# Output projection with tokens on partitions and 512 moving columns, row-sum norm, and the gate's products on DVE instead of PE

## The reference, cut to what matters

```
shift, scale, gate = split(c @ w_ada + b_ada, 3)          # c is one row of 1024; gate is one row of 1024
h = rmsnorm(x, g_pre) * (1 + scale) + shift
z_ssm, xbc, dt_raw, q, kv, nsa_gate, z_att, merge_gate = split(h @ w_in)
y_ssm = mamba2_branch(z_ssm, xbc, dt_raw, ...) @ w_ssm_out
y_nsa = nsa_branch(q, kv, nsa_gate, z_att, ...) @ w_nsa_out
mg = sigmoid(merge_gate)
merged = mg[0] * y_ssm + mg[1] * y_nsa
out = merged @ w_out                                      # 256 x 1024 times 1024 x 1024
return x + gate * rmsnorm(out, g_post)
```

## Time and profile before

| | |
|---|---|
| time of the timed runs | 501.9 us median of 3 (501.90, 499.15, 501.99) |
| profiled execution, first to last instruction | 498.6 us |
| PE busy | 456.4 us (92%), 3742 instructions |
| PE weight load busy | 417.5 us (84%) |
| DVE busy | 338.7 us (68%) |
| ACT busy | 272.5 us (55%) |
| POOL busy | 241.5 us (48%) |
| DMA | 83.0 MB, mean 166 GB/s |
| w_raw fetches | 133 of 512 KB, median 3.5 us from issue to landing |

### The profile page before, as it was taken

How to read it: one execution, slowest core, us unless ns; L and a number is a source line. 1 busy time by engine, 2 the same in 40 slices (tenths; PEclk the granted TensorE clock), 3 DMA queues, 4 the chain that set the end, 5 groups by cost and what they waited for, 6 DMA issues and landing times.

```text
span 498.6 us, 10047 instructions
## 1 busy us (share of the span) xinstructions
PE 456.4 (92%) x3742; PEld 417.5 (84%) x3742; DVE 338.7 (68%) x596; ACT 272.5 (55%) x531; POOL 241.5 (48%) x252
## 2 busy tenths in 40 slices
PE   0859999999999899988899999999999999999990
PEld 0439999989999799987788899889898989999990
DVE  0267989696989989888743586655556756457416
ACT  1264776563776476725574674745564656435441
POOL 1041544476673857894363552443544353344452
PEclk9988999999999999999999998999999999999996
DMA  8976445544433325327848863333433343465202
GB/s 323 423 300 221 153 146 162 178 129 152 144 128 128 124 88 185 118 81 268 318 162 271 305 214 106 110 108 128 143 113 128 128 148 109 145 237 172 81 1 84
DMA packets 21959, 83.00 MB, mean 166 GB/s; under 512 B 2444, under 2 KB 2834, under 8 KB 20626
## 3 DMA queue, kind: packets, MB, share of 16 engines
q1 hardware_dynamic: 21912, 82.37, 48.1%
HBM read 81.31 MB, written 1.05 MB: 165 GB/s over the span
## 4 chain that ended last, share of the span: by engine, by line
PE 66%; DVE 10%; DMA 8%; ACT 5%; issue 4%; POOL 4%; SPq 1%; ACTq 0%; DVEq 0%; POOLq 0%
PE gemm L600 18%; PE gemm L601 17%; PE gemm L602 17%; DMA w_raw<-in_wpack 8%; DVE w_lo L1090 3%; PE y_or_o L815 2%; ACT w_hi L841 2%; POOL cmp_blocks L462 2%; PE y_or_o L696 1%; PE score L778 1%; PE score L780 1%; SPq L475 1%; POOL w_lo L1381 1%; PE y_or_o L809 1%; PE score L671 1%
## 5 line engine op out<-in xcount | busy, mean ns | idle before, releaser
L1381 POOL TENSOR_TENSOR w_lo<-w_raw,w_hi 128x256 fp32r<-128x256 f32 (+1 forms) x117 | 134.4, 1153 | 162.6 <-ACT w_hi L841 154.6
L600 PE MATMUL gemm<-h_hi,w_hi 128*128 128x256 f32 x680 | 201.6, 296 | 4.5 <-DVE h_lo L1196 2.5
L601 PE MATMUL gemm<-h_lo,w_hi 128*128 128x256 f32 x680 | 194.2, 286 | 0.0
L602 PE MATMUL gemm<-h_hi,w_lo 128*128 128x256 f32 x680 | 194.0, 285 | 0.0
L1090 DVE TENSOR_TENSOR w_lo<-w_raw,w_hi 128x768 fp32r<-128x768 f32 (+1 forms) x117 | 130.3, 1116 | 68.9 <-ACT w_hi L841 68.6
L841 ACT CAST w_hi<-w_raw 128x1024 fp32r<-128x1024 f32 x117 | 122.1, 1044 | 45.9 <-PE gemm L602 30.0
L600 PEld LDWEIGHTS gemm<-h_hi,w_hi 128*128 128x128 f32 x680 | 132.2, 194 | 11.8 <-issue 10.1
L601 PEld LDWEIGHTS gemm<-h_lo,w_hi 128*128 128x128 f32 x680 | 132.3, 194 | 1.5 <-issue 1.0
L602 PEld LDWEIGHTS gemm<-h_hi,w_lo 128*128 128x128 f32 x680 | 132.1, 194 | 0.0
L1114 DVE SCALAR_TENSOR_TENSOR conv_acc<-gemm,conv_half,conv_acc 128x255 f32<-128x255 f32 (+2 forms) x72 | 34.5, 479 | 8.7 <-ACT conv_acc L863 6.9
L600 PE MATMUL gemm<-ynorm_hi,w_hi 128*128 128x256 f32 x128 | 36.5, 285 | 0.0
(11 more groups left out here) (235 smaller groups left out, 824.6 us busy)
## 6 DMA issues: line engine op xcount, KB each, us to landing
w_raw<-in_wpack SPq DMA_DIRECT2D x133, 512.0 KB, 3.5
w_ada_shift_scale<-in_w_ada SPq DMA_DIRECT2D x8, 1024.0 KB, 14.6
x_T<-in_xT SPq DMA_DIRECT2D x1, 1024.0 KB, 9.8
x_residual<-in_xT SPq DMA_DIRECT2D x1, 1024.0 KB, 5.5
out_T_dram<-out_T SPq DMA_DIRECT2D x4, 256.0 KB, 2.0
consts<-in_consts SPq DMA_DIRECT2D x1, 272.0 KB, 22.7
cmp_bias_and_valid<-in_cmp_bias SPq DMA_DIRECT2D x1, 272.0 KB, 5.8
w_compress<-in_w_compress SPq DMA_DIRECT2D x1, 192.0 KB, 6.4
```

What stands on the lines that cost most here:

```text
L600: nc.tensor.matmul(bank[:, 0:SEQ], w_hi, hi[:, k0 + k, :], start=first, stop=False)
L601: nc.tensor.matmul(bank[:, 0:SEQ], w_hi, lo[:, k0 + k, :], start=False, stop=False)
L602: last = nc.tensor.matmul(bank[:, 0:SEQ], w_lo, hi[:, k0 + k, :], start=False, stop=end)
L1381: nc.gpsimd.tensor_tensor(WL[:, n % LO_SLOTS, c:1024], RAW[:, u % RAW_SLOTS, c:1024], WH[:, n % HI_SLOTS, c:1024], ALU.subtract).then_inc( ...
```

## The change

Gate: the eight `ag` units are no longer multiplied on PE. DVE multiplies each unit by its column of `c` (one number per partition) and adds it into one tile `ada_gate_products` of 128 x 1024 (`ada_gate`). The ring slot of an `ag` unit is now free when DVE has done this. After the last one PE sums over partitions with eight matmuls of one moving column (step `agC`), POOL spreads gate_times_g over diagonals, and PE turns these with a matrix of ones into rows that are the same on every partition (step `agB`, two float32 matmuls of 512 columns, in the nsa stage). The order of the units becomes kw0 ag0 kw1 vs0 ag1 vs1 ag2 q0 ag3 q1 ag4 q2 ag5 q3 ag6 q4 ag7 q5 q6 q7.

Output: the merged activations are now stationary (128 tokens at a time) and w_out moves in 512 columns, so that tokens lie on partitions. The first half of the output columns (four units, k outermost) is accumulated for both token blocks t at once; the second half (four units) is done for t = 0 in full and then for t = 1. ACT squares a 128 x 512 bank and sums along the row in the same instruction; the norm is then one number per partition.

```diff
-    for n, kind in enumerate(("kw", "vs")):
-        for j in range(2):
-            units += [(kind, j, 0), ("ag", 0, 2 * n + j)]
-    for j in range(4):
-        units += [("q", j, 0), ("ag", 0, 4 + j)]
-    units += [("q", j, 0) for j in range(4, 8)]
+    units += [("kw", 0, 0), ("ag", 0, 0), ("kw", 1, 0), ("vs", 0, 0), ("ag", 0, 1), ("vs", 1, 0), ("ag", 0, 2)]
+    for j in range(5):
+        units += [("q", j, 0), ("ag", 0, 3 + j)]
+    units += [("q", j, 0) for j in range(5, 8)]
...
-    put(at(("ag", 0, 7)) + 1, ("agR", 0))
-    put(at(("ag", 0, 7)) + 3, ("agT", 0))
+    put(at(("ag", 0, 7)) + 2, ("agC", 0))
...
+    put(at(("nsa", 1, 0)), ("agD", 0))
+    put(at(("nsa", 4, 0)), ("agB", 0))
+    put(at(("nsa", 6, 0)), ("agB", 1))
...
                     if v in SPLIT_IDX:
                         sp.wait_ge(lo_ready, SPLIT_IDX[v] + 1)
                         sp.wait_ge(lo_rest_ready, SPLIT_IDX[v] + 1)
+                    elif UNITS[v][0] == "ag":
+                        sp.wait_ge(ag_done, UNITS[v][2] + 1)
                     else:
                         sp.wait_ge(native_mm, NATIVE_IDX[v] + 1)
...
+            def out_products(u, kk, t):
+                half, q = divmod(UNITS[u][1], 4)
+                n, k = SPLIT_IDX[u], OUT_K * q + kk
+                bank = (SB, TB)[half][t]
...
+                w_hi = WH[:, n % HI_SLOTS, OUT_N * kk:OUT_N * kk + OUT_N]
+                w_lo = WL[:, n % LO_SLOTS, OUT_N * kk:OUT_N * kk + OUT_N]
+                hi, lo = MH[:, k, P * t:P * t + P], ML[:, k, P * t:P * t + P]
+                nc.tensor.matmul(bank[:, :], hi, w_hi, start=(k == 0), stop=False)
+                nc.tensor.matmul(bank[:, :], hi, w_lo, start=False, stop=False)
+                return nc.tensor.matmul(bank[:, :], lo, w_hi, start=False, stop=(k == KT - 1))
...
                 if kind == "ag":
-
-                    if part == 0:
-                        wait_y_out(pe, ("y", 7))
-                    pe.wait_ge(w_in[u % RAW_SLOTS], 16 * (u // RAW_SLOTS + 1))
-                    for q in range(4):
-                        last = nc.tensor.matmul(YB[32 * q:32 * q + 1, 0:256], par("c", part, part + 1),
-                                                RAW[:, u % RAW_SLOTS, 256 * q:256 * q + 256], start=(part == 0), stop=(part == KT - 1))
-                    last.then_inc(native_mm, 1)
+                    return
+                if kind == "out":
+                    if j < 4:
+                        for kk in range(OUT_K):
+                            for t in range(2):
+                                last = out_products(u, kk, t)
+                        last.then_inc(unit_mm, 1)
                     return
...
+                elif what == "agC":
...
+                    pe.wait_ge(ag_done, KT)
+                    for m in range(KT):
+                        last = nc.tensor.matmul(bank[:, m:m + 1], AG[:, P * m:P * m + P], cst("ones", 0, 1), start=True, stop=True)
...
+            for t in range(2):
+                for q in range(4):
+                    for kk in range(OUT_K):
+                        last = out_products(UNITS.index(("out", 4 + q, 0)), kk, t)
+                last.then_inc(o_full, 1)
...
+            def square_out(half, t):
+
+                nc.scalar.activation(SQO[:, half, t, :], (SB, TB)[half][t][:, :], ACT.Square,
+                                     accum_out=SSO[:, half, t:t + 1]).then_inc(osq_done, 1)
...
+                if kind == "out":
+                    if j == 3:
+                        act.wait_ge(unit_mm, SPLIT_IDX[UNITS.index(("out", 3, 0))] + 1)
+                        for t in range(2):
+                            square_out(0, t)
+                        nc.scalar.activation(RO[:, 0, 0:1], EPSC[:, 1:2], ACT.Sqrt)
+                    return
...
+            def ada_gate(k):
+
+                u = UNITS.index(("ag", 0, k))
+                dve.wait_ge(w_in[u % RAW_SLOTS], 16 * (u // RAW_SLOTS + 1))
+                raw = RAW[:, u % RAW_SLOTS, :]
+                if k == 0:
+                    dve.wait_ge(native_mm, NATIVE_IDX[UNITS.index(("w1v", 0, 3))] + 1)
+                    nc.vector.tensor_scalar(AG[:], raw, par("c", 0, 1), None, ALU.mult).then_inc(ag_done, 1)
+                else:
+                    dve.wait_ge(ag_done, k)
+                    nc.vector.scalar_tensor_tensor(AG[:], raw, par("c", k, k + 1), AG[:], ALU.mult, ALU.add).then_inc(ag_done, 1)
...
                     if i + AHEAD in SPLIT_IDX:
                         split_lo(SPLIT_IDX[i + AHEAD])
+                    if UNITS[i][0] == "ag":
+                        ada_gate(UNITS[i][2])
...
+            for t in range(2):
+                gate_out(1, t)
+                dve.wait_ge(std_done, t + 1)
+                link(nc.vector.reciprocal(RO[:, t, 2:3], RO[:, t, 1:2]))
+                dve.wait_ge(og_done, 3 + t)
+                for n in range(2):
+                    cols = slice(OUT_N * n, OUT_N * n + OUT_N)
+                    nc.vector.scalar_tensor_tensor(OG[:, t, cols], OG[:, t, cols], RO[:, t, 2:3], XR[:, t, cols], ALU.mult,
+                                                   ALU.add).then_inc(fin_done, 1)
```

More of the change, by code:

```diff
@@ L135, in schedule @@
         put(max(last_h + 3, t0 + 8 + 4 * p), ("osp", p))
-    out0 = UNITS.index(("out", 0, 0))
-    for m in range(1, 7):
-        put(out0 + 1 + m, ("osum", m))
+    put(at(("nsa", 1, 0)), ("agD", 0))
+    put(at(("nsa", 4, 0)), ("agB", 0))
+    put(at(("nsa", 6, 0)), ("agB", 1))
     steps = []
@@ L156 @@
         NATIVE_IDX[_u] = len(NATIVE_IDX)
-    else:
+    elif _kind != "ag":
         SPLIT_IDX[_u] = len(SPLIT_IDX)
-    if _part == 0 and _kind != "ag":
+    if _part == 0 and _kind not in ("ag", "out"):
         TILE_IDX[(_kind, _j)] = len(TILE_IDX)
 SPLIT_UNITS = sorted(SPLIT_IDX)
-T_STEPS = ("dtT", "acs", "bt", "cb", "xt", "ea", "st", "ssq", "hidT", "kcp", "vcp", "vt", "cs", "ct", "pt", "agT")
+T_STEPS = ("dtT", "acs", "bt", "cb", "xt", "ea", "st", "ssq", "hidT", "kcp", "vcp", "vt", "cs", "ct", "pt", "agC")
 T_IDX, S_IDX, Y_IDX = {}, {}, {}
@@ L170 @@
         S_IDX[_s] = len(S_IDX)
-    if _s[0] in ("y", "pv"):
+    if _s[0] in ("y", "pv", "agB"):
         Y_IDX[_s] = len(Y_IDX)
@@ L214 @@
 H_POOL = (2, 4, 6)
-FINAL_DVE = 6
+OUT_K = 2
+OUT_N = 512
 AHEAD = LO_SLOTS - 1
@@ L505, in _ @@
                     wait_y_out(sp, ("pv", 7))
-                    sp.dma_start(XR[:], xT).then_inc(xr_in, 16)
-            for m, (who, value) in ((0, (0, 1)), (6, (1, 1)), (2, (0, 2)), (4, (0, 3))):
-                sp.wait_ge(fin_done[who], value)
-                sp.dma_start(out[:, m:m + 2, :], OUT[:, m:m + 2, :]).then_inc(out_done, 16)
+                    sp.dma_start(XR[:], x_tok).then_inc(xr_in, 16)
+            for n in range(4):
+                t, cols = n // 2, slice(OUT_N * (n % 2), OUT_N * (n % 2) + OUT_N)
+                sp.wait_ge(fin_done, n + 1)
+                sp.dma_start(out[:, t, cols], OG[:, t, cols]).then_inc(out_done, 16)
             sp.wait_ge(out_done, 4 * 16)
@@ L594, in weight_unit @@
                         pe.wait_ge(o_split, k + 1)
-                    if kind == "out" and j == 0:
-                        pe.wait_ge(ml_done, k + 1)
                     w_hi = WH[:, n % HI_SLOTS, P * k:P * k + P]
@@ L1064, in _ @@
                     nc.scalar.copy(KL[64:70], keys).then_inc(kl_alibi, 1)
-                elif what == "agR":
-                    wait_zeros(act, "rows2")
-                    act.wait_ge(native_mm, NATIVE_IDX[UNITS.index(("ag", 0, KT - 1))] + 1)
-                    for j in range(4):
-                        nc.scalar.copy(ROWS2[32 * j:32 * j + 1, :], YB[32 * j:32 * j + 1, 0:256]).then_inc(rows2_done, 1)
-            act.wait_ge(osq_full, 1)
-            nc.scalar.activation(RF[:, 0, :], YB[:, 0:SEQ], ACT.Sqrt, bias=EPSC[:, 1:2], scale=1.0 / D_MODEL).then_inc(rf_done, 1)
+                elif what == "agB":
+                    wait_y_full(act, step)
+                    nc.scalar.copy(GR[:, OUT_N * i:OUT_N * i + OUT_N], YB[:, :]).then_inc(y_free, 1)
+            for t in range(2):
+                act.wait_ge(o_full, t + 1)
+                square_out(1, t)
+                act.wait_ge(osq_done, 3 + t)
+                act.wait_ge(var_done, t + 1)
+                nc.scalar.activation(RO[:, t, 1:2], SSO[:, 1, t:t + 1], ACT.Sqrt, bias=RO[:, t, 0:1],
+                                     scale=1.0 / D_MODEL).then_inc(std_done, 1)
         @block.vector
@@ L1106, in read_out @@
                 kind, j = tile
+                if kind == "out":
+                    if j == 3:
+                        for t in range(2):
+                            gate_out(0, t)
+                    return
                 t = TILE_IDX[tile]
@@ L1572, in lay_out @@
             wpack[u] = ada[:, part, 2048:3072]
+        elif kind == "out":
+            wpack[u] = w_out[j]
         elif kind == "ssm":
```

125 lines of the change are left out of this document (58 added, 67 removed).

## The result

The changed kernel takes 522.56 us (median of 4 runs, 521.22 to 522.96), the kernel before 501.04 (499.15 to 501.99). The ratio is 1.0418, 95% interval 1.0382 to 1.0453. The profiled execution is 519.4 us long where that of before was 498.6: +20.8 us.

The account below looks back on a forecast made before the run. PE bounds most of the kernel; after the change a fetch loop without PE binds the ag stretch. Terms: 20.9 + 1.7 (agB) + 0 (output stage) - 7.2 (end) = +15.4, on the median 517 us, range 509 to 525.

Parts of the forecast that it names:

- The loop: Ag stretch: each ag's products wait for the previous ag's slot, then fetch, rounding, split; q7's gemm comes 20.9 us later.
- The fetch: Term of one loop round: first fetch of a pair on an otherwise quiet queue, 3.7 us.
- the six rounds: From ag1 to ag7: issue 0.1, fetch 3.7, rounding 1.1, split 1.5, products 1.1; 7.5 us each.
- The start: Ahead of the rounds: ag0's products end near 255.0 us, ag1's at 264.6.
- rival 2: Ag stretch: the products are not held up by POOL; round 7.0 us, +12, 514 us; 20 in 100.
- the amount: DVE's extra work, 8 to 9 us where DVE has 20 us free: its amount is harmless, its place is not.
- rival 3: Ag stretch: PE's clock falls; rounds stay, q5, first scores and q6 end near 314; +4, 521 us; 25 in 100.
- The output stage: Output units: matmuls 22.1 us, PE waits 1.0 for the last split; 23.0 us in all, change 0.
- The end: Behind the last gemm: 5.7 us for t = 1 alone instead of 12.9, so -7.2.

Follow-up runs that it names:

- 1: Changed kernel with DVE's products of an ag unit put ahead of the split of the unit three further on: 503.18 us, ratio 1.0027.
- 2: Changed kernel with DVE's products of an ag unit put two steps earlier, ahead of the read-outs too: 496.36 us, ratio 0.9881.
- 5: Changed kernel with DVE's seven accumulating products done on 128 of 1024 columns, order and fetches unchanged: 517.43 us, ratio 1.0319.
- Experiment 6: Changed kernel with filler matmuls of unread result on PE, five at ag0 and eight at each other ag step: 518.04 us, ratio 1.0337.
- 9: Output half of the change alone, with the last output unit's cast and split put ahead of the squares and table load: 495.21 us, ratio 0.9881.
- Experiment 3: Changed kernel with the gate put back as before (matvecs, transposes, unit order), so only the output half: 495.58 us, ratio 0.9875.

## Why the prediction was right, and where its sizes were off

The forecast was 517 us, range 509 to 525; 522.56 lies in it, 5.6 above the point. Step by step:

**The loop.** Right, and shown: 1 shortens the loop and 2 takes it off the path, both by order alone; 5 shortens only its DVE part. The last products end at 309.73 (forecast 309.6), agC takes 1.77 us (1.7), q7's gemm starts at 311.64 (311.3). This agreement is partly luck, for two terms were off against each other:

- *The fetch.* "3.7", taken from a fetch of the kernel before, measured 3.22 to 3.37 in the six rounds. The row was taken from a stretch with 247 GB/s, and the rounds move 142 (265.6 to 310 us). The kernel before has the same 142 GB/s from 330 to 462 us, and there the median fetch took 3.3 us: that was the nearer row. All else in the round held: rounding 1.05 (1.1), split and products together 2.64 (1.5 + 1.1). So 7.05 instead of 7.5, and 2.7 us less over six rounds.
- *The start.* ag1's products end at 267.4, not 264.6. With ag0's matvecs gone, PE has nothing between kw0 and the compression, and its clock falls to the lower level (1.2 GHz: the granted clock is 0.50 from 255.3 to 260 us). In PE's timeline:

```profile
252.53 0.29 PE L752 MATMUL small<-w_compress,hid_v_T 128*128 128x64 f32 x1 [2.10 <-ACT hid_v_T L1045]
...
255.23 0.56 PE L621 MATMUL gemm<-h_hi,w_hi 128*128 128x256 f32 x1
```

kw1's gemm, which starts there, takes 5.11 us instead of 2.9, so what PE leaves for ACT comes late, and ACT's rounding for ag1's round starts only at 263.68. The prediction had looked for a falling clock later, at q5, and not at the first gap. Experiment 6 fills the gap, has 2.95 us there, and its first accumulating products come 2.4 us earlier.

**Held up by POOL (rival 2).** The forecast's side was right. The products take 1.75 us beside POOL's split and 1.27 without it (experiment 2), and they end 1.08 us behind POOL's end at 273.33. That the round came out at rival 2's 7.0 is the fetch's doing. The change adds 13.0 us of work to DVE (0.74 and seven times 1.75), where the prediction had 8 to 9; it made no difference, as the prediction said of the amount. The Trainium skill, SBUF — State Buffer, section "🔬 SBUF: two separate sides", says that a DVE instruction with two SBUF inputs and a GpSimd one that reads SBUF exclude each other for the whole instruction; the trace agrees, the 128-column products of experiment 5 with their 0.82 us too.

**The clock (rival 3).** The clock fell, as this rival has it, and the time came out near its 521, but not by its path. The q gemms in the rounds take about 4.5 us each instead of the 6 it had, and the last of them, q5's (4.41 us), and q6's behind it, at full clock, still end before the last products (309.57 against 309.73), so nothing is lost there. What the clock cost is the late start, which the shorter fetches hid, and some 1.3 us of what follows q7.

**Behind q7.** This step was missing: the prediction took the delay at q7 as carried on unchanged. It grew by 4.7 us, through PE's wait of 3.2 us for ACT's exponentials behind the 5.72-us fetch, and some 1.3 us by the lower clock after it (the gemm behind the scores begins with matmuls 0.21 us apart instead of 0.12). Most of the 5.6 us between forecast and result lies here.

**The output stage.** Forecast 23.0, measured 23.6. The matmuls start 0.233 us apart, as forecast from the rows (0.23). The 216 ns that the prediction quotes from the Trainium skill, TensorE: Matmul & The Clock Gate, section Back-to-back issue gap, is there the gap of a matmul by itself; for a stream with weight loads the section gives 131 ns, and the measured 233 don't agree. The table load and the small root took what they were given, and the two squares with their row sums 1.3 us instead of 1.6, in ACT's timeline after the change:

```profile
501.80 0.60 ACT L875 ACTIVATE out_sq<-score 128x512 f32<-128x512 f32 x1 [1.70 <-PE score L570]
...
503.08 1.28 ACT L889 ACT_TABLE_LOAD   x1
...
504.49 1.03 ACT L864 CAST w_hi<-w_raw 128x1024 fp32r<-128x1024 f32 x1
```

and PE's wait was 0.8 us (forecast 1.0), shown by 9 in the trace. agB came out at 1.6 (forecast 1.7).

**The end.** Forecast 5.7, measured 5.4. In the timeline the row sum, the root and the reciprocal of one column, and two multiply-adds stand one behind the other:

```profile
514.02 0.60 ACT L875 ACTIVATE out_sq<-small 128x512 f32<-128x512 f32 x1 [4.58 <-PE small L570]
514.75 0.29 ACT L1102 ACTIVATE rstd_out<-out_sq_sums,rstd_out 128x1 f32<-128x1 f32 x1
515.35 0.15 DVE L1401 RECIPROCAL rstd_out<-rstd_out 128x1 f32<-128x1 f32 x1
515.54 1.41 DVE L1405 SCALAR_TENSOR_TENSOR out_tok<-out_tok,rstd_out,x_residual 128x512 f32<-128x512 f32 x2
```

They answer to the table load, the 256-column reciprocal and the rounds of out_T of the earlier trace rows. Experiment 3 has this half by itself: 0.9875 where 0.990 was expected.

## What to carry over

When the consumer of a prefetched buffer changes engine, ask first which instruction now gives the slot back, what stands ahead of it in that engine's order, and whether one of those waits for a later fetch of the same ring; such a loop costs the full latency of a fetch each round, however idle the engines are. The amount of work moved says nothing about it: here the same work cost 27 us in one place (against the output half alone), and under 1 two steps earlier. Spreading the units out does not cut such a loop: fetches in strict order carry the wait on to the next unit, and the loss shows only when the lead is used up. And an engine that takes over work leaves a gap on the one that had it: count what steps were placed by that engine's work, and what runs behind the gap.

## What the runs showed of the hardware that was not expected

- A gap of 2.10 us on PE, and short matmuls behind it, were followed by the lower clock level (1.2 GHz): a gemm of 24 matmuls took 5.11 us instead of 2.95. With matmuls whose result nobody reads in the idle places of the ag steps the kernel took 518.0 us instead of 522.6 (experiment 6).
- A fetch of 512 KB, first on a queue that had run empty, took 3.22 to 3.37 us in the six rounds, and 5.72 in a burst.
- A DVE product of two SBUF tensors over 1024 columns took 1.27 us alone and 1.75 beside POOL's split; for 128 columns, beside POOL's split, still 0.82.
